# Four-byte moving operands stored in four quarters of a row and read by turns

## What is computed

```python
h = rms_norm(x, g)                    # 512 x 1024
z = h @ w_in                          # 1024 x 8192 in the first block: 64 column tiles of 128
... attention on parts of z -> oa, ob
merged = gates0 * (oa @ w_a) + gates1 * (ob @ w_b)
x = x + rms_norm(merged @ w_out, g2)
gu = rms_norm(x, g3) @ w_gate_up      # 1024 x 5632
x = x + rms_norm((silu(g) * u) @ w_down, g4)   # 2816 x 1024
```

## Time and profile before

| | |
|---|---|
| median of 3 runs | 3235.04 us |
| lowest and highest | 3233.91, 3241.21 us |
| span of the profiled execution | 3232.1 us |
| PE busy | 3169.8 us, 98% |
| DVE, ACT, POOL busy | 43%, 42%, 42% |
| matmuls at line 464 (in `gemm`) | 11,472 of 15,912 |

### The profile page before, as it was taken

One profiled execution on the slowest core, in us unless ns is written; L12 is line 12 of the kernel. 1 busy time (PEld: TensorE's weight loads), 2 busy tenths in 40 slices (PEclk: granted clock), 3 DMA queues, 4 the chain that ended last, 5 costly groups with the idle time before them and its releaser, 6 DMA issues. The chain is left out here.

```text
span 3232.1 us, 45316 instructions
## 1 busy us (share of the span) xinstructions
PE 3169.8 (98%) x15912; PEld 2537.2 (78%) x15912; DVE 1388.0 (43%) x2604; ACT 1347.7 (42%) x2111; POOL 1349.9 (42%) x685
## 2 busy tenths in 40 slices
PE   9999999999999999999999999999999999999999
PEld 7778888788887778888788876777888867778887
DVE  5743335555416733335555424953112148531211
ACT  6765554322227765563322224453222245532222
POOL 3233333444443233334444443544444534444444
PEclk9999999999999999999999999999999999999999
DMA  3222222355522122222355523212323232122232
GB/s 142 65 75 89 88 88 79 118 187 196 183 95 87 60 87 79 84 88 91 121 198 183 181 87 113 73 34 80 96 96 104 96 114 66 40 78 97 97 102 87
DMA packets 93595, 333.28 MB, mean 103 GB/s; under 512 B 10864, under 2 KB 12080, under 8 KB 93232
## 3 DMA queue, kind: packets, MB, share of 16 engines
q1 hardware_dynamic: 91760, 325.52, 29.6%
q10 hardware_dynamic: 1728, 6.36, 0.5%
HBM read 329.69 MB, written 8.44 MB: 105 GB/s over the span
## 5 line engine op out<-in xcount | busy, mean ns | idle before, releaser
L440 POOL TENSOR_TENSOR wLo<-wring,wHi 128x1024 fp32r<-128x1024 f32 x482 | 1163.3, 2414 | 1703.1 <-ACT wHi L418 1702.9
L464 PE MATMUL psG<-hHi,wHi 128*128 128x512 f32 x2992 | 1183.4, 396 | 5.8 <-ACT whole L1913 2.0
L464 PE MATMUL psG<-hLo,wHi 128*128 128x512 f32 x2992 | 1169.9, 391 | 9.7 <-POOL hLo L489 8.7
L464 PE MATMUL psG<-hHi,wLo 128*128 128x512 f32 x2992 | 1165.4, 390 | 0.0
L418 ACT ACTIVATE wHi<-wring 128x1024 fp32r<-128x1024 f32 x482 | 510.1, 1058 | 959.9 <-PE psG L464 952.7
L464 PEld LDWEIGHTS psG<-hHi,wHi 128*128 128x128 f32 x2992 | 562.1, 188 | 143.4 <-issue 29.1
L464 PEld LDWEIGHTS psG<-hLo,wHi 128*128 128x128 f32 x2992 | 561.5, 188 | 141.3 <-POOL hLo L489 24.0
L464 PEld LDWEIGHTS psG<-hHi,wLo 128*128 128x128 f32 x2992 | 562.6, 188 | 113.4 <-issue 0.5
L464 PE MATMUL psG<-hidLo,wHi 128*128 128x512 f32 x704 | 273.9, 389 | 0.0
L464 PE MATMUL psG<-hidHi,wHi 128*128 128x512 f32 x704 | 273.9, 389 | 0.0
L464 PE MATMUL psG<-hidHi,wLo 128*128 128x512 f32 x704 | 273.9, 389 | 0.0
(11 more groups left out here) (332 smaller groups left out, 3265.0 us busy)
## 6 DMA issues: line engine op xcount, KB each, us to landing
wring<-in_w SPq DMA_DIRECT2D x490, 512.0 KB, 3.3
modw<-in_wmod SPq DMA_DIRECT2D x96, 512.0 KB, 5.5
e_copies<-e_rows ACTq DMA_DIRECT2D x8, 512.0 KB
T_tab<-e_copies SPq DMA_DIRECT2D x4, 1024.0 KB, 5.6
mask<-in_mask SPq DMA_DIRECT2D x2, 1536.0 KB, 6.0
xin_sb<-in_x SPq DMA_DIRECT2D x4, 512.0 KB, 5.3
e_copies<-e_rows ACTq DMA_DIRECT2D x8, 256.0 KB
out<-o_sb SPq DMA_DIRECT2D x4, 512.0 KB, 3.4
```

Source lines behind the costliest of these rows:

```text
L440: pool.tensor_tensor(wLo[:, c % CUTS, :, :], wring[:, c % RING, :, :], wHi[:, c % CUTS, :, :], ALU.subtract).then_inc(w_cut[c % CUTS], 1)
L464: mm = pe.matmul(psG[:, G.slot(u), :], w[:, c % CUTS, k, :], r(j), start=start and j == 0 and n == 0, stop=stop and j == len(kts) - 1 and ...
```

## The change

Two helpers give two views of a row of 512 words:

```diff
+        def by_turns(a):
+            return a.rearrange("p (h n) -> p n h", h=4)
+        def in_fours(a):
+            return a.rearrange("p (n h) -> p n h", h=4)
+        def pairs(src):
+            return lambda j: in_fours(src(j))
+        def words(a, first=0):
+            return lambda j: by_turns(a[:, first + j, :])
```

```diff
-                    h = tiles(hHi), tiles(hLo)
+                    h = words(hHi), words(hLo)
...
-                            gemm(pe, g_AB + 2 * j, CH1_AB + j, (tiles(oaHi), tiles(oaLo)), range(4), ...)
+                            gemm(pe, g_AB + 2 * j, CH1_AB + j, (words(oaHi), words(oaLo)), range(4), ...)
...
-                    high_act(act, 0, kept(whole), tiles(hHi), KT, tmp_full, h_high)
+                    high_act(act, 0, pairs(kept(whole)), words(hHi), KT, tmp_full, h_high)
...
-                    rest_pool(pool, 0, tiles(whole), tiles(hHi), tiles(hLo), KT, h_high, h_full)
+                    rest_pool(pool, 0, pairs(tiles(whole)), words(hHi), words(hLo), KT, h_high, h_full)
...
-                            dve.tensor_tensor(hLo[:, j, :], kept(whole)(j), hHi[:, j, :], ALU.subtract).then_inc(hd_full, 1)
+                            dve.tensor_tensor(by_turns(hLo[:, j, :]), in_fours(kept(whole)(j)), by_turns(hHi[:, j, :]), ALU.subtract).then_inc(hd_full, 1)
...
-                        act.activation(oaT[:, i, :], psG[:, G.slot(u), :], ACT.Copy).then_inc(G.emptied(u), 1)
+                        act.activation(by_turns(oaT[:, i, :]), in_fours(psG[:, G.slot(u), :]), ACT.Copy).then_inc(G.emptied(u), 1)
...
-                        act.activation(obT[:, i, :].rearrange("p (t r) -> p r t", r=DL),
-                                       psG[:, G.slot(in_DL(13, i)), :].rearrange("p (r t) -> p r t", r=DL), ACT.Copy).then_inc(...)
+                        act.activation(obT[:, i, :], psG[:, G.slot(in_DL(13, i)), :], ACT.Copy).then_inc(...)
...
-                            did(dve.tensor_copy(hidHi[:, k, :], hid))
-                            dve.tensor_tensor(hidLo[:, k, :], hid, hidHi[:, k, :], ALU.subtract).then_inc(hid_full, 1)
+                            did(dve.tensor_copy(by_turns(hidHi[:, k, :]), in_fours(hid)))
+                            dve.tensor_tensor(by_turns(hidLo[:, k, :]), in_fours(hid), by_turns(hidHi[:, k, :]), ALU.subtract).then_inc(hid_full, 1)
```

More of the change, by code:

```diff
@@ L820, in project_second @@
                         def project_second(d, c):
-                            gemm(pe, g_DA + d, CH1_DA + c, (tiles(hHi, half), tiles(hLo, half)), range(half, KT), i, GK_DA, 4, start=False)
+                            gemm(pe, g_DA + d, CH1_DA + c, (words(hHi, half), words(hLo, half)), range(half, KT), i, GK_DA, 4, start=False)
                         def scores(n):
@@ L891, in tile_second @@
                         def tile_second(j, c, k):
-                            gemm(pe, in_DL(j, i), CH1_DL + c, (tiles(hHi, k), tiles(hLo, k)), range(k, KT), i, GK_DL, 12, start=False)
+                            gemm(pe, in_DL(j, i), CH1_DL + c, (words(hHi, k), words(hLo, k)), range(k, KT), i, GK_DL, 12, start=False)
                         def turn_v(n, ring, ps, u, K):
@@ L972, in _ @@
                         for j in range(4):
-                            gemm(pe, g_AB + 2 * j, CH1_AB + j, (tiles(oaHi), tiles(oaLo)), range(4), i, 8, 4, ready=None if j else both(counted(o_high), counted(o_rest)))
-                            gemm(pe, g_AB + 2 * j + 1, CH1_AB + j, (tiles(obHi), tiles(obLo)), range(4, 8), i, 8, 4, ready=None if j else both(counted(o_high, DA_HEADS), counted(ob_rest)))
+                            gemm(pe, g_AB + 2 * j, CH1_AB + j, (words(oaHi), words(oaLo)), range(4), i, 8, 4, ready=None if j else both(counted(o_high), counted(o_rest)))
+                            gemm(pe, g_AB + 2 * j + 1, CH1_AB + j, (words(obHi), words(obLo)), range(4, 8), i, 8, 4, ready=None if j else both(counted(o_high, DA_HEADS), counted(ob_rest)))
                     with pe.Fori(0, 2) as i:
@@ L995, in _ @@
                                 ks = range(8) if part < 2 else range(FT - 16)
-                                gemm(pe, g_DN + j, CH1_DN + 3 * j + part, (tiles(hidHi, 8 * part), tiles(hidLo, 8 * part)), ks, i, 4, 12,
+                                gemm(pe, g_DN + j, CH1_DN + 3 * j + part, (words(hidHi, 8 * part), words(hidLo, 8 * part)), ks, i, 4, 12,
                                      start=part == 0, stop=part == 2, ready=None if j else both(*[counted(hid_full, 2 + 8 * part)] * 2))
@@ L1232, in _ @@
                     act.preload_act_table(ACT.Silu)
-                    high_act(act, 2 * KT, kept(whole), tiles(hHi), KT, tmp_full, h_high)
+                    high_act(act, 2 * KT, pairs(kept(whole)), words(hHi), KT, tmp_full, h_high)
                     act.wait_ge(cb_in, 16)
@@ L1269, in _ @@
                     add_branch(branch_1, KT)
-                    rest_pool(pool, KT, tiles(whole), tiles(hHi), tiles(hLo), KT, h_high, h_full)
+                    rest_pool(pool, KT, pairs(tiles(whole)), words(hHi), words(hLo), KT, h_high, h_full)
                     cut_rests(pool, CH1_GU + CUTS, CH1)
@@ L1666, in second_half @@
                     def second_half(name):
-                        gemm(pe, g[name], CH2_Z + z_pos[name], (tiles(hHi, half), tiles(hLo, half)), range(half, KT), start=False)
+                        gemm(pe, g[name], CH2_Z + z_pos[name], (words(hHi, half), words(hLo, half)), range(half, KT), start=False)
                     def turn_values(name):
@@ L1857, in _ @@
                         at = 2 * (j % 4)
-                        gemm(pe, g[f"rest{j}"], CH2_WR + j // 4, (tiles(hHi, REST_K[0]), tiles(hLo, REST_K[0])), (at, at + 1))
+                        gemm(pe, g[f"rest{j}"], CH2_WR + j // 4, (words(hHi, REST_K[0]), words(hLo, REST_K[0])), (at, at + 1))
                         if j >= 1:
```

26 lines of the change are left out of this document (13 added, 13 removed).

## The result

| | median | runs from | to | span of the profiled execution |
|---|---|---|---|---|
| before | 3235.34 us | 3233.91 | 3241.21 | 3232.1 us |
| after | 3870.86 us | 3855.74 | 3876.35 | 3869.8 us |

The ratio is 1.1955, with a 95% interval of 1.193 to 1.198. The kernel became 635 us slower. The forecast was 3126 us, faster; the wide range (to 5650) holds the time, its own range of the first case (3095 to 3195) doesn't.

The account below looks back on a forecast made before the run. PE's own instructions, mostly gemm's products, were taken to bound the kernel. 3232.1 - 134 + 20 + 5 = 3123 us of span, 3126 us as median; range 3090 to 5650 us, the first case's own 3095 to 3195.

Parts of the forecast that it names:

- the first case: Products in gemm lose the excess over the array's rate, at least in good part: 3126 us, range 3095 to 3195, chance 0.48.
- What bounds the kernel: PE is busy 98% of the span; 11,472 matmuls of gemm at 226.7 ns make 2601 us, 80% of it.
- What the step is made of: Each gemm product needs 215.0 ns by the array's rate; the other 11.7 ns suggest a limit in delivering moving words.
- the first rival: Products of gemm stay at 226.7 ns and only the edges count: 3260 us likeliest, chance 0.17.
- the lower end: A gemm product at 215.0 ns, if reading by turns from four places removes all delivery cost: 134 us less.
- The term of the products: The new view's effect on gemm's 11,472 products, between 215.0 and 913 ns each; taken as 134 us less.
- The halved rate: Rival: each moving word in gemm takes one cycle of 1.2 GHz, 428.3 ns a product, 5573 us, chance 0.22.
- the full strided price: Rival: every moving word in gemm pays as ACT's strided write, 913 ns a product, about 11,130 us, chance 0.13.
- Edges of 20 + 5 us: Strided writing of hHi and hLo after eight norms adds 20 us; PE waiting more for DVE on other pieces adds 5.
- The hidden layer: DVE's strided writes of hidden rows, 3.6 in place of 2.1 us a row, are covered by products and cost nothing.
- The weight cuts: ACT's and POOL's cut of the weights, 3.5 us together, stays covered by products, 5.16 or 3.87 us.
- The clock doesn't fall: PE's clock holds, since PE is as busy as before; no time was added.

Follow-up runs that it names:

- one_word: The kernel before, with gemm's moving operand reading the first word of the row 512 times: 3128.95 us.
- two_turns: The kernel before, with gemm's moving operand read by turns from two halves of the row, 256 words apart, rows stored plainly: 3114.21 us.
- reads_only: The kernel before, with gemm's moving operand read by turns from four quarters and every row stored in plain order: 3846.87 us, ratio 1.1883.
- step_four: The kernel before, with gemm's moving operand read at steps of four words (0, 4, 8 to 508, then 1, 5 and so on): 5881.56 us.
- within_piece: The kernel before, with gemm's moving operand read in blocks of four words in the order 0, 2, 1, 3: 3233.28 us.
- whole_pieces: The kernel before, with gemm's moving operand read as four neighbouring words from each quarter of the row in turn: 3688.36 us.
- near_two: The kernel before, with gemm's moving operand read in blocks of 8 words, by turns from the two groups of four in each: 3113.64 us.
- writes_only: The changed kernel with its strided writes and reads on ACT, DVE and POOL kept, but PE reading moving rows in plain order: 3267.22 us, ratio 1.0105.
- halves_plain_writes: The changed kernel with two halves for four quarters, writers following storage order with the step on their source (obT still written strided): 3120.52 us, ratio 0.965 against before.

## Why the prediction was wrong

**What bounds the kernel** was right: only the step of the products mattered. 613 us of the 638 come with the reading alone.

**What the step is made of** was right. The reasoning from the plain float32 rows gave 215.0 ns for the array's own rate and put 11.7 ns of each product down to the delivery of the moving words. `one_word` and `two_turns` stand at 216.9 and 216.2 in the same quotient in which plain order has 226.9. A different order of words can take nearly all of it away: 120 us of span. So the first rival, "the rate stays 226.7", is refuted as a mechanism: most of the excess is not the array's hand-over, nor weight loads in the way.

**The step that failed** is the choice of the lower end for the products: "a reader that can hold four pieces has each of its pieces used up completely". Two places by turns behave like that, at 4 words as at 256; four don't. The term of the products was put at -134 us; by the step of 283.3 ns it is +650, of which the span shows 613 in `reads_only`. The bounds (215 and 913) held, but the value taken between them rested on no row. The prediction said so ("a choice with little behind it") and still gave it 0.48. That the text called four pieces a number the reader "can hold" was the whole of the bet, and no row before the change bears on any number of places. That two places do give the saving doesn't make the bet half right: nothing in the prediction told two from four.

**The rivals with a dearer word** had the sign right and the size wrong. The halved rate (428.3 ns) and the full strided price (913 ns) were for a view in which every word pays. With four places, part is paid: the measured 283 ns is 226.7 x 5/4, which is noted and not explained. With eight places (486.9) and at steps of four (460.2) each word does pay, 0.95 and 0.90 ns, a little above the 0.83 ns of a column of plain float32: that is the size of the halved-rate rival, 428.3 ns, and half of the 1.78 ns that a word costs ACT. The rule of the Trainium skill, "Advanced Engine Details and Errata", section "Memory Cachelines", that SBUF is read in lines of 16 bytes and each access to another line pays, was right in its warning and agrees with `step_four`, with `within_piece` and with the sign of the loss by four places. `whole_pieces` changes from one group of four to another just as often as plain order and costs 41 ns a product more (268.3 against 226.9), which the rule doesn't give. And `near_two` and `two_turns` go to another group of four words at every word and are 10.7 ns a product cheaper than plain order, where the section has a penalty. In both the measurement decides.

**The writers.** ACT came to 1135 ns, a little above its upper bound of 1116, which was taken from another strided view. A DVE row took 697 + 1064 + 1067 ns = 2.8 us, within the 3.6 allowed. POOL came to 1557, about halfway between its old 1293 and the 1.8 us expected, and ACT's copy to `oaT` to 1.07 us. Edges of 20 + 5 us were forecast, `writes_only` shows 33 us (bounds 0 to 55). PE's wait for `hLo` was to grow to some 25 us; it came to 18.4 with the old step, and 14.4 in the kernel after, whose longer step probably hides a part. The hidden layer cost nothing that the waits show. The weight cuts stayed covered; at the forecast step they would have been so a little less, as in `halves_plain_writes` PE waits 2.6 us for `wLo`, 1.2 before. "The clock doesn't fall" held only roughly: its mean was 0.995 after and 0.993 in `writes_only`, where it is an estimated 13 of the 33 us, and the sum had no term for it.

**The range of the first case** doesn't follow from its own words. All of the excess gone and nothing at the edges is 3235 - 134 = 3101 us, not 3095. Half of it gone and the edges at their bounds is 3235 - 67 + 55 = 3223, not 3195. Neither changes that the measured 3871 us lies far outside.

**What stays open.** The table above isn't explained by one rule. Shown is: two places by turns are as cheap as one word read 512 times; the number of places decides far more than their distance; eight neighbouring words taken together cost almost as little as a plain row, four don't. Why four neighbours from two halves stand at 250 and from four quarters at 268, why sixteen neighbours aren't cheaper than eight, and what makes the ratio of 5/4, no run here tells. All numbers of places and all distances tried are powers of two; three places, or places at another distance, were not tried, so a cost that comes from how addresses at such distances meet is not ruled out.

## What to carry to other kernels

A matmul's step above what its columns need (here 226.7 against 215 ns) is worth a test of the moving view alone: one edit at the matmul, with a wrong order of tokens, tells the rate before any writer is touched. A writer that makes PE wait can cost more than the wait: here the products that followed ran for a while at the lower clock. Where the only support for a choice is a number (four places) that no row bears on, the neighbours of that number (two, eight) belong into the same experiment, since here the sign turned between two and four. When data must be stored in another order, let the writer follow the order of storage and take its source with the step: it kept DVE and POOL at about their old times, and was 23 us better than strided writing.

## What the runs showed of the hardware

- Two places read by turns deliver fp32r words faster than a plain row: 216.2 against 226.9 ns for 512 columns, on 11,472 products 120 us of span.
- With no change in what is multiplied, a product's price went from 216 to 487 ns with the order of the same 512 words, and four words left together are not enough to be cheap: four neighbours from each quarter took 268.3 ns, eight 232.4 (some 1 ns of it from a lower clock at the start).
- Writing 512 words by turns to the four quarters of a row cost ACT 502 ns more, DVE 376, POOL 264. A source at steps of two words cost ACT 164 ns from `branch` in SBUF and nothing from `psS` in PSUM; it cost DVE nothing from `psS`, and POOL 13 ns from `branch`.
- Writing rows with a stride doesn't matter to a reader that takes them in plain order: 226.9 ns in `writes_only`.
- After waits of 0.8 and 0.6 us between short groups of products, PE's granted clock was 0.57 from 2886 to 2890 us of `writes_only`, and products started 0.43 us apart instead of 0.23.
